# Running product of the RWKV decays by a multiplying scan and a reciprocal, in a one-core hybrid encoder layer

## What is computed

```python
p = xn @ w_in[l]                              # 2048 -> 6400 columns
w = -jax.nn.softplus(-(w0 + jnp.tanh(w_lo) @ w2)) - 0.5
decay = jnp.exp(-jnp.exp(w))                  # per frame and channel, 0 < decay < 1
...
def rwkv7_step(state, inp):
    r, w, k, v, a, b = inp
    sa = jnp.einsum('bhvk,bhk->bhv', state, a)
    state = (state * w[:, :, None, :] + sa[..., None] * b[:, :, None, :]
             + v[..., None] * k[:, :, None, :])
```

## Time and profile before

| | |
|---|---|
| median of 3 runs | 989.14 us (989.1 to 989.64) |
| profiled execution | 989.14 us |
| its span, first to last instruction | 986.9 us |
| around the span | 2.2 us |
| TensorE busy | 959.3 us, 97% of the span |
| VectorE busy | 441.3 us, 45% |
| ScalarE busy | 279.0 us, 28% |
| granted TensorE clock, mean | 0.996 |

### The profile page before, as it was taken

The page is one execution under the profiler, slowest core; times in us unless marked ns, Lnnn a source line. Parts: engine busy times, 40 slices in busy tenths (PEclk is TensorE's granted clock), DMA queues, the critical chain, the costliest instruction groups (busy, mean ns, idle before and its releaser), DMA issues.

```text
span 986.9 us, 18210 instructions
## 1 busy us (share of the span) xinstructions
PE 959.3 (97%) x8062; PEld 741.3 (75%) x8062; DVE 441.3 (45%) x695; ACT 279.0 (28%) x451; POOL 73.7 (7%) x81
## 2 busy tenths in 40 slices
PE   5999999999999999999999999999999999999995
PEld 5999999999999999988887656566565656566552
DVE  3748947444556567674433132241413223141314
ACT  4555543222336556545530010000101000010003
POOL 5010003223000000520000000000000000000000
PEclk9999999999999999999999999999999999999998
DMA  9785544224244444699986999999999999999992
GB/s 270 201 259 171 171 129 129 88 88 129 89 128 135 144 143 134 235 311 401 342 339 264 402 399 429 426 428 428 424 430 426 426 428 427 427 427 428 424 394 109
DMA packets 85009, 285.79 MB, mean 290 GB/s; under 512 B 5900, under 2 KB 57176, under 8 KB 71616
## 3 DMA queue, kind: packets, MB, share of 16 engines
q1 hardware_dynamic: 80896, 279.98, 73.7%
q0 software_dynamic: 1824, 4.04, 1.6%
q10 hardware_dynamic: 2208, 0.57, 0.3%
HBM read 280.36 MB, written 4.22 MB: 288 GB/s over the span
## 4 chain that ended last, share of the span: by engine, by line
PE 88%; DVE 5%; ACT 2%; DMA 2%; issue 1%; POOL 1%; DVEq 0%; SPq 0%; ACTq 0%; POOLq 0%
PE bank L1319 23%; PE bank L930 23%; PE bank L1341 10%; PE bank L1291 6%; PE bank L947 3%; PE bank L949 3%; PE bank L948 3%; PE bank L883 2%; PE bank L1301 2%; PE bank L1360 1%; DVE ring_r L1518 1%; PE bank L1302 1%; PE bank L1046 1%; DMA arena<-in_x 1%; PE bank L1218 1%
## 5 line engine op out<-in xcount | busy, mean ns | idle before, releaser
L930 PE MATMUL bank<-xTr,hi 128*128 128x256 f32 x1344 | 249.1, 287 | 1.9 <-DVE ring_r L1518 1.7
L1319 PE MATMUL bank<-arena 128*64 128x256 f32 x2048 | 232.3, 381 | 1.0 <-DVE arena L1921 1.0
L1518 DVE TENSOR_TENSOR ring_r<-arena,hi 128x1024 fp32r<-128x1024 f32 x132 | 163.5, 1250 | 129.1 <-ACT hi L609 127.2
L930 PEld LDWEIGHTS bank<-xTr,hi 128*128 128x128 f32 x1344 | 208.8, 191 | 8.5 <-issue 4.5
L1319 PEld LDWEIGHTS bank<-arena 128*64 128x64 f32 x2048 | 144.5, 137 | 82.1 <-issue 15.0
L930 PE MATMUL bank<-xTr,ring_r 128*128 128x256 f32 x672 | 189.9, 283 | 0.0
L609 ACT ACTIVATE hi<-arena 128x1024 fp32r<-128x1024 f32 x132 | 139.0, 1061 | 112.1 <-PE bank L930 78.8
L930 PEld LDWEIGHTS bank<-xTr,ring_r 128*128 128x128 f32 x672 | 128.6, 191 | 0.0
L1341 PE MATMUL bank<-arena,const 128*64 128x512 f32 x448 | 100.8, 597 | 0.0
L1917 DVE TENSOR_TENSOR arena<-arena,bank 128x512 f32<-128x512 f32 x60 | 63.9, 1111 | 40.6 <-PE bank L1302 40.6
L1341 PEld LDWEIGHTS bank<-arena,const 128*64 128x64 f32 x448 | 30.3, 137 | 54.5 <-issue 52.0
(11 more groups left out here) (309 smaller groups left out, 937.1 us busy)
## 6 DMA issues: line engine op xcount, KB each, us to landing
arena<-in_expert_w_up SPq DMA_DIRECT2D x30, 2048.0 KB, 20.6
arena<-in_expert_w_gate SPq DMA_DIRECT2D x29, 2048.0 KB, 22.4
arena<-in_w_in SPq DMA_DIRECT2D x50, 1024.0 KB, 5.3
arena<-in_expert_w_down SPq DMA_DIRECT2D x24, 2048.0 KB, 21.1
arena<-in_w_out SPq DMA_DIRECT2D x16, 1024.0 KB, 7.5
arena<-in_expert_w_down SPq DMA_DIRECT2D x14, 1024.0 KB, 13.1
arena<-in_expert_w_gate SPq DMA_DIRECT2D x6, 1024.0 KB, 6.4
arena<-in_expert_w_up SPq DMA_DIRECT2D x4, 1024.0 KB, 9.3
```

Of the source, the lines that this page charges most:

```text
L930: ins = MM(PJ[n % 2][:, h * U:(h + 1) * U], a, b, start=h + q + tt + k == 0, stop=h == 1 and q == 3 and tt == 3 and k == 2)
L1319: ins = MM(bank[7 if last and st_ else 2 + st_][CAP * a:CAP * a + CAP, c // 2 * U:(c // 2 + 1) * U], xg[:, t, CAP * a:CAP * a + CAP], slot ...
L1518: TT(ring_r[:, n % 2, q, :], ring[:, n % 2, q, :], hi[:, g % NHI, :].bitcast(f32), ALU.subtract).then_inc(s["lo_done"], 1)
```

## The change

The decays are now multiplied, not added as logarithms. ScalarE exponentiates `decay` in place (L658 of the changed kernel, after VectorE's new signal `decay_done`), VectorE copies the 16 chunk starts of it into the otherwise zero `chunk_start`, zeroes them in `decay`, and runs the scan as state × decay + chunk_start, which leaves `Pc` itself. `Pprev` is a shifted copy of `Pc`, on ScalarE, one unit later; `Pinv` is four reciprocals on VectorE. ScalarE's three exponentials go, an exponential and a copy come. The scan stands 3 granules' splits later in VectorE's text. At the second place one `split_lo(1)` moves behind the `yTr` subtraction.

```diff
@@ ScalarE
             keep(3)
+            act.wait_ge(s["decay_done"], 1)
+            step(A_(decay, decay, ACT.Exp), s["scan_ready"])
             step(A_(lam[:, 2:4], lam[:, 0:2], ACT.Exp), s["lam_exp"])
-            act.wait_ge(s["kr_done"], 2)
-            flat = [t.rearrange("p a b -> p (a b)") for t in (Pprev, Pinv, Pc)]
-            step(A_(flat[0][:, 1:], flat[2][:, 0:AT * SEQ - 1], ACT.Exp), s["scan_ready"])
-            advance(1)
-            step(A_(flat[1], flat[2], ACT.Exp, scale=-1.0), s["scan_ready"])
-            advance(1)
-            step(A_(flat[2], flat[2], ACT.Exp), s["scan_ready"])
+            advance(2)
             act.wait_ge(s["kkn_ps"], 1)
...
             keep(4)
+            act.wait_ge(s["kr_done"], 2)
+            copy(Pprev.rearrange("p a b -> p (a b)")[:, 1:], Pc.rearrange("p a b -> p (a b)")[:, 0:AT * SEQ - 1], s["scan_ready"])
             advance(3)
@@ VectorE
-            flat = [t.rearrange("p a b -> p (a b)") for t in (decay, chunk_start, Pc)]
-            step(V.memset(chunk_start, 1.0))
-            step(V.memset(flat[1][:, 0::CH], 0.0))
+            step(V.memset(chunk_start, 0.0))
             v.wait_ge(s["lora_ev"], 8)
-            step(TS(decay, decay, -0.5 * DECAY_C, -0.5 * DECAY_C, ALU.mult, ALU.add))
-            step(V.tensor_tensor_scan(flat[2], flat[1], flat[0], 0.0, ALU.mult, ALU.add), s["kr_done"])
+            step(TS(decay, decay, -0.5 * DECAY_C, -0.5 * DECAY_C, ALU.mult, ALU.add), s["decay_done"])
             split_lo(1)
             step(TS(iclr, iclr, 0.5, 0.5, ALU.mult, ALU.add))
             split_lo(1)
             mix(3)
             split_lo(1)
-            split_lo(2)
+            flat = [t.rearrange("p a b -> p (a b)") for t in (decay, chunk_start, Pc, Pprev, Pinv)]
+            v.wait_ge(s["scan_ready"], 1)
+            step(V.tensor_copy(flat[1][:, 0::CH], flat[0][:, 0::CH]))
+            step(V.memset(flat[0][:, 0::CH], 0.0))
+            split_lo(1)
+            step(V.tensor_tensor_scan(flat[2], flat[0], flat[1], 0.0, ALU.mult, ALU.add), s["kr_done"])
+            split_lo(1)
             v.wait_ge(s["knorm_done"], 2)
...
-            v.wait_ge(s["scan_ready"], 3 + AT)
+            v.wait_ge(s["scan_ready"], 2 + AT)
...
             split_lo(1)
-            step(V.memset(flat[1][:, 0::CH], 1.0))
-            split_lo(3)
+            v.wait_ge(s["scan_ready"], 2)
+            step(V.memset(flat[3][:, 0::CH], 1.0))
+            split_lo(1)
+            for c in range(AT):
+                step(V.reciprocal(Pinv[:, c, :], Pc[:, c, :]))
+                if c == 1:
+                    split_lo(1)
+            split_lo(1)
             mix(6)
@@ VectorE, second place
             scale_gate(1)
-            split_lo(1)
             for m in range(NM):
                 v.wait_ge(s["yhi_done"], m + 1)
                 step(TT(yTr[:, 1, 0:4, m * P:(m + 1) * P], K[4 + m][:, :].rearrange("p (c n) -> p c n", c=4),
                         yTr[:, 0, 0:4, m * P:(m + 1) * P].bitcast(f32), ALU.subtract), s["ylo_done"])
-            split_lo(1)
+            split_lo(2)
             normalise(0)
```

More of the change, by code:

```diff
@@ L234, in build @@
             sq1_done diag0_done diag1_done halves_zero knorm_done prep var_ready rstd_done xt_ready xhi_done xlo_done
-            pool_ones tanhA sgA lora_ps lora_ev kkn_ps g_ev scan_ready
+            pool_ones tanhA sgA lora_ps lora_ev kkn_ps g_ev decay_done scan_ready
             prep_done nat_ps nat_ev gram_ps gram_ev n_ev bon_ps bon_ev ct_done t1_ps t1_ev xu_ps xu_ev
```

## The result

| | before | after |
|---|---|---|
| median | 989.14 us (5 runs, 988.72 to 989.87) | 998.45 us (5 runs, 995.63 to 999.86) |
| ratio, 95% interval | | 1.0095 (1.0083 to 1.0107) |
| profiled execution, its span | 989.14, 986.9 us | 1000.01, 998.2 us |

The change is slower, by 9.3 us. That is inside the range (993.0 to 999.0) and on the side forecast; the point, 996.1, is 2.35 us too low, and outside the likeliest case's own range of 995.2 to 997.0. The executions lie 4 us apart, these five of the kernel before 1 us; in the larger samples beside the experiments those of the kernel before lie 1.6 to 2 us apart, but for one at 992.98 and one in a slow state at 1207.46.

A forecast was written before the change was run, and what follows sets the result against it. TensorE was taken to bound the kernel, with VectorE and ScalarE costing time only where it waits for them. The terms −0.25 + 4.25 + 3.2 − 0.2 = +7.0 us on 989.14 gave 996.1 us, range 993.0 to 999.0.

The forecast's parts named there:

- the likeliest case: Whole kernel: the waits come as reckoned and the clock stays at full, 995.2 to 997.0 us, chance 0.70.
- What bounds the kernel: Whole kernel: TensorE, busy 97% of the span; VectorE and ScalarE matter only where TensorE waits for them.
- Term 1: Before granule 17: with the scan moved, its split comes earlier and TensorE's wait goes, −0.25 us.
- Term 2: ScalarE: three exponentials become one and a copy, hidden with 2.7 us to spare; effect nothing.
- Term 3: Four reciprocals on VectorE delay splits and preparation; TensorE waits before granules 29, 30, 31 and the bonus matmuls, +4.2 us.
- Term 4: Second place: granule 68's split behind the `yTr` subtractions starts that granule 3.2 us late, 0.2 us comes back, net +3.0 us.
- Nothing takes it back: After granule 68: the expert loads follow TensorE, so the stream shifts with it and the loss stays.
- the rival of the expert stream: Expert part: waiting for weights swallows the later start, up to 7 us gained back, 989.3 us, chance 0.04.
- The clock: Gap before granule 68: the clock falls to half speed, up to 2.7 us more, 998.8 us, chance 0.12.
- the likeliest sum: Whole kernel: −0.25 + 4.25 + 3.2 − 0.2 = +7.0 us, giving 996.1 us, with no fall of the clock.

The follow-up runs named there:

- e6: The kernel before with only its own logarithmic scan moved behind granule 17's split: 989.72 us, ratio 1.0004.
- e10: The kernel before with only the bonus term's multiplications moved past three splits: 987.21 us, ratio 0.9979.
- e2: The kernel before with only the second place changed (granule 68's split behind the `yTr` subtractions): 993.7 us, ratio 1.0044.
- e4: The changed kernel with the second place put back and the four reciprocals replaced by copies of the same shape: 988.22 us, ratio 0.9989.
- e8: e1 with the first two reciprocals right behind the scan, the other two ahead of `split_lo(2)` and `mix(6)`: 989.7 us, ratio 1.0005.
- e1: The changed kernel with the second place put back (granule 68's split again ahead of the `yTr` subtractions): 993.64 us, ratio 1.0043.
- e5: The whole changed kernel with 4, 1, 3 and 8 dummy matmuls before granules 30, 31, the bonus matmuls and granule 68: 995.38 us, ratio 1.0061.
- e9: e8 with the bonus term's multiplications moved behind granules 28 to 30: 991.76 us, ratio 1.0029.
- e11: e9 with 3 dummy matmuls on TensorE ahead of its wait for the preparation: 989.64 us, ratio 1.0003.
- e7: The kernel before with the scan moved as in e6 and the bonus term's multiplications moved past three splits: 987.77 us, ratio 0.9984.

## Why the prediction was right, and where it fell short

**What bounds the kernel: right.** TensorE's queue is full, and what counts is who is late for it. All of the loss is TensorE waiting or TensorE slowed.

**Term 1 (−0.25): right, and its condition went unsaid.** The wait before granule 17 went, which is 0.34 us from the low-rank matmuls to the key norms. To the start of granule 27 the trace shows −0.5 us, of which 0.1 was there by 34 us already, before the changed part. The step took what follows to shift along with TensorE. e6, which has the same 0.34 us and loses 0.46 behind them, shows that this holds only because the exponentials are gone, so that the table load does not wait for the scan. The step also took the 0.25 us of one execution for the size of that wait; 0.8 and 1.0 us stand in the traces of e10 and e2.

**Term 2 (nothing): right**, and e4 shows it: with the copy and the new waits in place, nothing is lost.

**Term 3 (+4.2): right.** The sum by starts is 4.2; 1.76 us for a reciprocal, and the preparation's last operation at 128.79 for the 129 forecast. e8 adds what the term doesn't say: it is a price of the place. With two of the four in 2.9 us of VectorE's idle time TensorE takes 48.21 us from the key norms to the bonus matmuls, with all four late 51.14, without them (e4) 46.98: 1.2 us in place of 4.2.

**Term 4 (+3.0): right.** 3.3 us from the transposes' end to granule 68, forecast 3.2; alone it costs 4.5 with the clock (e2).

**Nothing takes it back: right.** From granule 68 to the end the kernel is 1.2 us slower, of the loss about 0.5 us is regained and not 7, and the rival of the expert stream falls.

**The clock: the step that failed.** It was a rival with a chance of 0.12, and only for the gap before granule 68; in the profiled execution it came true there and at a place not named, the bonus matmuls. The wait before granule 68 ended at 305.36 and not at the 302.4 forecast, because the first fall had come before it. The term missing from the likeliest sum is 1.7 us for the second place, and 0 (e1's trace) to 3.4 for the first: the median is 3.1 us over what e5 shows with the clock held. The price was too high for the one place (2.7 forecast, 1.7 measured) and zero for the other, so the rival's total of 998.8 is near 998.45 partly by chance. The 2.7 was taken from the start of the kernel, by counting matmuls per us; the row used for that, 12 to 13 us in the earlier trace rows, has a granted clock of 1.00, so it doesn't show half speed by itself. That the median lies inside the range, 0.55 us under its upper end, is partly luck too: the likeliest sum lacked 3.1 us of the clock, and 0.4 us around the span, which no term had, came back. Why it failed: I weighed gaps by their length alone, and looked for the longest. The forecast itself put a wait of 1.35 us right ahead of the bonus matmuls, 16 of them with 2 columns each in 1.84 us, and such a place, a wait with small matmuls and transposes behind it, was in no row of the kernel before. That it would leave the clock alone was taken over from waits between granules.

The Trainium skill, page "TensorE: Matmul & The Clock Gate", section "Why this matters for your kernels", warns against idle gaps over a certain length between bursts of matmuls. For the gap of 3 us e2's trace agrees with it: the clock fell at the end of it. For the fall near 131 us the rule, which speaks of a gap's length alone, does not point to the place: the wait there is 1.18 us long, shorter than the 1.57 before granule 30 that left the clock alone. There the measurement decides, e9 with e11.

## What to carry to other kernels

When the busiest engine is fed by another, cost an edit by a walk through the feeder's queue from the last point at which it was idle to the next hand-over. Seven us of elementwise work cost 4 us on TensorE here, then 1.2 when half of it stood in the idle time, and one split moved behind a wait cost 3.3, or 4.5 with the clock. After that, look at the granted clock right behind each new wait, also a short one: here 1.17 us ahead of the small bonus matmuls cost 1.7 us more. A few dummy matmuls ahead of the wait gave it back, where they were no longer than the wait; size them from a row that shows the whole group.

## What the runs showed of the hardware

In these traces the granted clock does not fall by gap length alone. TensorE's wait of 1.12 us ahead of granule 27 was followed by no fall in nine traces, and 1.57 ahead of granule 30 by none in two (e1 and the changed kernel). Ahead of the 16 bonus matmuls of 2 columns, 1.17 was followed by one in e9, and 1.18 in the changed kernel's trace but not in e1's. At the 3.03 us ahead of granule 68 it fell in both traces that have them (e2 and the changed kernel). Each fall lasted 3.4 us, the one near 131 us in the changed kernel 6.8. e1 shows that the same wait at the same place comes with and without the fall, which fits the changed kernel's spread of 4 us and the clocks of its executions.

The time around the span was 2.2 us for the kernel before, e2 and e6, and 1.8 for the others. It doesn't follow the form of the scan (e7 and e10 have the old one); what sets it stays open. Whoever compares medians to 0.5 us has to compare the spans too.

Also open is how often each of the two falls occurs in the changed kernel, since only the profiled execution shows the clock over time; the others have its mean alone.
